# Where VectorE combines the two softmax maps of differential attention within a slot

## The reference

```python
def diff_attend(q, k, v, lam, scale):
    s = jnp.einsum('bqhjd,bkhjd->bhjqk', q, k).astype(jnp.float32) * scale
    p = jax.nn.softmax(s, axis=-1)
    attn = p[:, :, 0] - lam * p[:, :, 1]
    return jnp.einsum('bhqk,bkhe->bqhe', attn.astype(v.dtype), v)
```

## Time and profile before

| | |
|---|---|
| median of 3 runs | 2605.39 us (2604.3 to 2608.54) |
| the profiled execution | 2604.3 us, its span 2602.5 us |
| mean granted TensorE clock | 0.977 |
| PE busy | 2403.0 us, 92% of the span |
| DVE, ACT busy | 1346.5 us (52%), 997.2 us (38%) |
| slots of layer 0, first scores to last combine | 175.9 to 361.3 us |
| slots of layer 1, the same | 825.1 to 979.0 us |

### The profile page before, as it was taken

One profiled execution on the slowest core, in us unless ns is written; L12 is line 12 of the kernel. 1 busy time (PEld: TensorE's weight loads), 2 busy tenths in 40 slices (PEclk: granted clock), 3 DMA queues, 4 the chain that ended last, 5 costly groups with the idle time before them and its releaser, 6 DMA issues. The chain is left out here.

```text
span 2602.5 us, 48850 instructions
## 1 busy us (share of the span) xinstructions
PE 2403.0 (92%) x20344; PEld 1893.0 (73%) x20344; DVE 1346.5 (52%) x2145; ACT 997.2 (38%) x1669; POOL 161.0 (6%) x213
## 2 busy tenths in 40 slices
PE   7999999888979999888989979999999989999997
PEld 5777678777857666777666657788787667788786
DVE  5346544566365653556476664455424665455423
ACT  3225443444343444454355554222223454222221
POOL 0000000442000000243000000000000010000000
PEclk9999999999999999999999989999999999999999
DMA  7721111000212111100221112233233222333232
GB/s 273 254 65 33 33 46 57 11 5 12 60 31 72 41 49 53 34 5 12 66 81 57 57 33 73 83 96 96 87 94 110 63 59 73 89 97 96 86 96 70
DMA packets 299970, 182.58 MB, mean 70 GB/s; under 512 B 5226, under 2 KB 284412, under 8 KB 299660
## 3 DMA queue, kind: packets, MB, share of 16 engines
q1 hardware_dynamic: 286364, 150.50, 19.7%
q10 hardware_dynamic: 12480, 25.17, 2.7%
q0 software_dynamic: 944, 4.27, 0.5%
HBM read 177.80 MB, written 2.12 MB: 69 GB/s over the span
## 5 line engine op out<-in xcount | busy, mean ns | idle before, releaser
L245 DVE TENSOR_TENSOR wlo<-wraw,whi 128x1024 fp32r<-128x1024 f32 (+1 forms) x276 | 334.3, 1212 | 397.3 <-ACT whi L238 377.6
L238 ACT ACTIVATE whi<-wraw 128x1024 fp32r<-128x1024 f32 (+1 forms) x276 | 287.4, 1043 | 268.9 <-PE PW L311 255.8
L399 PE MATMUL PW<-hhi,whi 128*128 128x512 f32 (+1 forms) x880 | 325.0, 369 | 11.7 <-DVEq L3104 7.0
L309 PE MATMUL PW<-hhi,whi 128*128 128x512 f32 (+1 forms) x840 | 323.6, 385 | 8.6 <-DVE wlo L245 8.6
L310 PE MATMUL PW<-hhi,wlo 128*128 128x512 f32 (+1 forms) x840 | 323.3, 385 | 0.0
L311 PE MATMUL PW<-hlo,whi 128*128 128x512 f32 (+1 forms) x840 | 322.9, 384 | 0.0
L400 PE MATMUL PW<-hhi,wlo 128*128 128x512 f32 (+1 forms) x880 | 307.2, 349 | 0.0
L401 PE MATMUL PW<-hlo,whi 128*128 128x512 f32 (+1 forms) x880 | 306.9, 349 | 0.0
L399 PEld LDWEIGHTS PW<-hhi,whi 128*128 128x128 f32 x880 | 168.4, 191 | 57.4 <-issue 23.9
L309 PEld LDWEIGHTS PW<-hhi,whi 128*128 128x128 f32 x840 | 159.6, 190 | 40.8 <-issue 9.5
L400 PEld LDWEIGHTS PW<-hhi,wlo 128*128 128x128 f32 x880 | 168.8, 192 | 22.0 <-issue 3.3
(11 more groups left out here) (447 smaller groups left out, 4391.6 us busy)
## 6 DMA issues: line engine op xcount, KB each, us to landing
wraw<-in_w_in SPq DMA_DIRECT2D x68, 512.0 KB, 3.9
mod_w<-in_mod_w ACTq DMA_DIRECT2D x12, 2048.0 KB, 11.6
wraw<-in_ffn_w_gate SPq DMA_DIRECT2D x44, 512.0 KB, 3.8
wraw<-in_ffn_w_up SPq DMA_DIRECT2D x44, 512.0 KB, 3.8
wraw<-in_ffn_w_down SPq DMA_DIRECT2D x32, 512.0 KB, 3.9
wraw<-in_attn_w_in SPq DMA_DIRECT2D x24, 512.0 KB, 3.9
wraw<-in_w_out SPq DMA_DIRECT2D x16, 512.0 KB, 3.9
wraw<-in_rg_w_in SPq DMA_DIRECT2D x16, 512.0 KB, 3.9
```

What stands on the lines that cost most here:

```text
L238: act.activation(whi[:, slot, 0:kb, :], wraw[:, slot, 0:kb, :], ACT.Copy).then_inc(S("w_hi"), 1)
L245: dve.tensor_tensor(wlo[:, slot, 0:kb, :], wraw[:, slot, 0:kb, :], whi[:, slot, 0:kb, :].bitcast(F32), ALU.subtract).then_inc(S("w_split"), 1)
L309: pe.matmul(acc, whi[:, u % 2, k, :], rhi[:, k0 + k, s0:s1], start=a, stop=False)
L399: e.matmul(acc, whi[:, u % 2, k, :], rhi[:, k0 + k, s0:s1], start=k == 0, stop=False)
```

## The change

Two lines are added to `dve_program` of the attention phase. `dve_combine` of step i is no longer called at "first", behind `dve_max`, but at "second":

```diff
                     elif name == "first":
                         if i < ns:
                             dve_max(v, i)
+                    elif name == "second":
+                        if i < ns:
                             dve_combine(v, i)
                     elif name == "sums":
                         dve_normed(v, i, x)
```

## The result

The changed kernel is slower: the median of its runs is 2629.12 us (2625.36 to 2631.2) against 2605.12 before, a ratio of 1.008 with a 95% interval of 1.0065 to 1.0094. The median is that of four runs taken beside the kernel before; over all 21 runs of the changed kernel on record (2619.73 to 2631.2) it is 2627.14 us. The profiled execution took 2625.89 us, its span is 2624.1, against 2602.5.

A forecast was written before the change was run, and what follows sets the result against it. PE, busy 92% of the span, was taken as the bound, so only its waits cost. Layer 0's 13.9 and layer 1's 10.0 us, 24.0, on 2604.3 gave 2628.3; with the median 1.1 higher, 2629 us, range 2618 to 2637.

The forecast's parts named there:

- That the idle time isn't filled: DVE's 83.3 us idle ahead of the combine becomes longer idle time before the split, whose ACT input follows the exps.
- Slot 6: Layer 0: combine ends 3.63 us later against 1.9 us to spare; PE waits 1.74 us, the slot costs 1.77.
- The other slots of layer 0: Same steps at the other slots' rows, 0.25 to 1.76 us each where late; layer 0 costs 13.9 us in all.
- Layer 1: Rotary block and split precede the combine in slots 1, 5, 9; PE waits 3.2 us in slot 5; layer costs 10.0 us.
- The sum: Both layers' attention slots: 13.9 + 10.0 = 24.0 us more, time 2629 us; restarts of PE at most 0.25 us each.
- The sign: Whole kernel: slower 0.90, same 0.06, faster 0.04; L1221 waits for the combine some 20 times, 20 to 28 us.
- The clock: Rival, 13%: waits of 3.2 us in layer 1's slots 5 and 9 lower PE's clock, 1.7 us each, 2632 to 2633.
- No change, and faster: Rivals: combine still ahead of its transposes, 2605 us, 6%; idle time really filled, down to 2594 us, 4%.

The follow-up runs named there:

- whi_ahead: Changed kernel, but ACT does each slot's first two dense chunks ahead of the exps and L1326 stays behind the combine: 2601.18 us, 0.9994 of before.
- spare_slots: Kernel before with the combine moved only in slot 20 of layer 0 and slots 0, 4, 8, 12 of layer 1: 2601.93 us, 0.9996 of before.
- only_layer1: Kernel before with the combine moved to the second half of the slot in layer 1 only: 2613.87 us, 1.0041 of before.
- transposes_later: Changed kernel with the first-half transposes L1221 and their evacuation L1276 put one chunk ahead of "second": 2624.03 us, 1.0099 of before.
- before_transposes_later: Kernel before, combine at "first", with the first-half transposes L1221 and evacuation L1276 one chunk ahead of "second": 2604.95 us, 1.0025 of before.

## Why the prediction was right

- **That the idle time isn't filled.** It held. The idle time ahead of the combine fell from 83.3 to 15.1 us and came back ahead of L245, L1326 and L1332, 92.6 us for 68.2. whi_ahead shows the cause: with ACT's part ahead of the exps the same DVE order, but for L1326, costs nothing.
- **Slot 6.** Forecast a wait of 1.74 us and a cost of 1.77; the wait was 1.82. Slots 8, 10, 12, 14 and 16 waited 2.02, 1.49, 1.84, 2.02 and 1.49.
- **The other slots of layer 0.** Slots 2 and 4 waited 1.17 and 1.50, forecast 1.11 and 1.42. Slot 21 waited 1.30 where 0.88 was forecast, the largest miss of a single wait in layer 0.
- **Layer 1.** Forecast waits of 3.2 us in slots 5 and 9: both 3.27 (idle time of the weight loads, as forecast; the matmuls stood 2.85 us). The 1.2 us forecast for slot 6 were 0 there and 1.72 in slot 10, the largest misses of single waits. The pairs cost 2.7 each all the same, as forecast; the scores' old waits absorb the difference. Slots 0, 4, 8 and 12 cost nothing, and spare_slots tests them with slot 20 alone.
- **The sum.** 24.0 us forecast (13.9 and 10.0 are 23.9), 24.0 between the medians, 22.9 in the slots of the profiled execution, 22.0 from the median of all 21 runs. The agreement of the first two to a tenth is luck: by its interval the ratio says 17 to 24.5 us. The bound of 0.25 us for a restart of PE stood on no row; the one measured in slot 6 is 0.05.
- **The sign.** Some 20 waits of 20 to 28 us in total were forecast: 19 of the weight loads came, with 30.9 us, and 17 of the matmuls, with 23.0.
- **The clock.** It was given as a rival at 13% with 1.7 us for each wait of 3.2. The windows behind slot 5 and behind slot 9 of layer 1, first in the changed kernel and then in only_layer1, read (granted clock third from the end)

```profile
901.70:905.00 3.30, 3.27 (x12) 2.25 (x13) 2.01 (x4) 2.58 (x6) 0.00 (x0) 0.59 0.33 99
...
945.10:949.00 3.90, 3.90 (x28) 3.42 (x29) 1.96 (x4) 3.16 (x7) 0.00 (x0) 1.00 0.26 78
```

```profile
888.80:892.80 4.00, 4.00 (x31) 3.52 (x30) 1.76 (x4) 3.46 (x7) 0.00 (x0) 1.00 0.21 63
...
932.00:936.00 4.00, 4.00 (x18) 2.97 (x19) 1.91 (x4) 2.92 (x6) 0.00 (x0) 0.66 0.25 76
```

  So the clock did fall, to 0.59 over 3.3 us and 0.66 over 4.0 us, so the level of 1.2 GHz for most of each, behind one of the two waits in each profile, not always the same one. What I had wrong is the price. Slots 4 to 7 of the changed kernel, with the fall, cost 2.68 us, and slots 8 to 11, without it, 2.70; in only_layer1 it is 2.66 without and 3.06 with it. PE's slower work runs while it would have waited in the next slot: slot 6's transposes, forecast to wait again, didn't after the fall, and waited 1.72 in slot 10 without it. The rival was half right, a mechanism that occurs and, in these two profiles, costs 0 to 0.4 us.
- **No change, and faster.** Both needed the combine to keep ahead of its transposes, or `whi` to be ready before the exps end. Neither held in the changed kernel; the second was brought about in whi_ahead.

What the forecast didn't see is that a late DVE can reach PE by a second way. It followed the maximum only for the scores of the next step, and transposes_later shows that with the transposes moved the lateness comes back through the evacuation, nearly whole in layer 1 and in part in layer 0. In the changed kernel itself this way isn't taken: the waits of L1221 for L1276 are 0.8 us, as before.

## What to carry to other kernels

Moving a waiting instruction behind others fills its idle time only if those others are ready by then; look up what each of them waits for, and where that stands in the other engine's order. Here everything that was put ahead of the combine waited for ACT work behind the very exps that the combine waited for, so the idle time of DVE grew. Compute the spare time of the moved result (here 1.9 us to the transposes) and compare it with the shift (3.6 us); where the spare time is larger, the move is free. The idle time is worth filling with work whose input is old, and the instruction to free from a queue ahead of it is the one that leads to what the busiest engine waits for, here the maximum, for whose exps the scores wait.

## What the runs showed of the hardware

How long PE stood did not settle whether its clock fell. In layer 1 the matmuls stood 2.85 us (the weight loads 3.27 or 3.28) between dense stretches and were followed by a granted clock of 1.00 in two cases and of 0.59 and 0.66 in two others, in the same two places of the same code. In transposes_later the granted clock over the 4 us behind waits of 2.84 and 2.73 us (layer 0) and 1.70 us (layer 1) was 0.57, 0.62 and 0.62, but 1.00 behind one of 3.07 us and another of 1.70; in before_transposes_later it was 0.67 behind 2.66 us, and 1.00 and 0.63 behind two waits of 2.14 us. So the 1.00 behind the 1.77 us of the earlier trace rows doesn't say that such a wait is safe.

A restart of PE after DVE's result took 0.05 us (235.89 to 235.94), as little as its restart after ACT's exps in the kernel before (196.85 to 196.90).
